# Reordered roundings, clips and turns in an expert stage, with its weights loaded in 2 MB DMAs

## The chip, the cores and the metric

The kernel runs on one core of a Trainium2 chip. The metric is the device time of the whole program in microseconds (us), the median of several runs.

## The reference, cut to what matters

One layer of a hybrid encoder on 512 tokens of width 1024, in float32. Three token mixers (differential attention, an mLSTM, a cross-attention into 256 memory tokens) are gated, projected and added; then comes a mixture of experts, the part that the change touches:

```python
h = h + mix @ w_out
xt = rms_norm(h)                                  # (512, 1024)
top_v, top_i = lax.top_k(xt @ router_w + router_b, 4)     # 4 of 32 experts for each token
top_w = softmax(top_v)
h1 = ragged_dot(xt[tok], w_gate_up) + b_gate_up   # each expert: 1024 x 2048
gate, up = minimum(h1[:, :1024], 7), clip(h1[:, 1024:], -7, 7)
a = (up + 1) * gate * sigmoid(1.702 * gate)
y = (ragged_dot(a, w_down) + b_down) * top_w      # each expert: 1024 x 1024
out = h + segment_sum(y, tok)
```

Each expert has 12 MB of weights, all 32 together 384 MB. Each must be read once from HBM.

## The kernel before, in words

The mixers and their projections fill the first half of the time (`stage_prep` to `stage_mix`) and are the same in both kernels but for the first expert loads. `stage_moe` (L2179) does the experts, one after the other.

**Order of the experts.** The router's counts sort the experts into seats: `KINDS_OF` (L61) says for each place in the sequence whether it is big (0, up to 128 tokens) or small (1, up to 64 tokens). Place 0 and place 31 are big; between them stand 15 pairs, a small one and then a big one (`pairs`, L2526). Expert numbers are read from `K.order` at run time.

**Units.** The weights of an expert are cut into 12 units of 1 MB, [128 x 2048] float32, at the positions `pos` 0 to 3 (up), 4 to 7 (down), 8 to 11 (gate). For each position there is one slot in SBUF, `moe_raw` (L2962), so 12 slots hold exactly one expert's amount. The slots 0 and 1, 2 and 3, and so on are neighbours in SBUF (`homes`, L2960).

**Small experts** use a slot as it is: `small_unit` (L2301) multiplies in full float32, two column halves of 64 tokens at a time, straight from `moe_raw`.

**Big experts** are split: ScalarE rounds a unit to float32r into `moe_hi` (`hi`, L2230, a ring of six), VectorE writes the remainder over the raw slot as `moe_lo` (`lo`, L2237), and TensorE does three products for each piece (`unit`, L2285): 12 matmuls of 512 columns a unit. So each unit of a big expert needs first ScalarE, then VectorE, then TensorE. The split units of a big expert are counted by `off` 0 to 11 in the order of use: up 0 to 3, gate 4 to 7, down 8 to 11 (`place`, L2252).

**Order on each engine**, written out by hand. TensorE, for an expert n (`small`, L2578, and `big`, L2595): the up units of n; behind the second of them the turn (transpose) of the activations `a` of expert n-1 (`turn_a`, L2383); the down units of n-1; the gate units of n; behind the second of them the turn of the gathered rows of n+1 (`turn_x`, L2330). ScalarE (L2670 to L2694): in `small` the Silu of expert n-1, rounding 8 of it, `keep_a_hi` (the rounded turned activations), roundings 9 to 11, the weighting of y, `keep_x_hi` of the next expert and its roundings 0 and 1; in `big` the Silu of the small expert before it, `keep_a_small` (L2458), roundings 2 to 5, the weighting, rounding 6, `keep_x_small` (L2412), rounding 7. VectorE (L2817 to L2840) follows with swiglu, remainders, and `clip` (L2428), which frees the banks of the up product.

**Loads.** SP (`refill`, L2537) goes through the positions in the order 0 to 11, which is the order in which TensorE uses them. For each it waits until the unit in the slot has been used (`s_use`, counted by TensorE once a unit), and loads the next 1 MB (`load`, L2225): rows of 8 KB, one for each of the 128 partitions. Positions 0 to 3 and 8 to 11 are loaded for expert n+1, positions 4 to 7 for expert n, whose down part comes one expert later. Each slot has a semaphore of its own. The first four units are loaded by `stage_mix` at L1727, the others of the first expert at L1734.

**Gather and scatter.** POOL gathers the rows of the next expert from HBM (`fetch`, L2489) and adds the weighted results into the output with an indirect DMA (`late`, L2507).

The first wait of `keep_a_small`, for TensorE's turn of `a`, and what stands behind it on ScalarE:

```python
def keep_a_small(act, n):
    act.wait_ge(s_aT, START + n * 2 + 2)
...
    silu(act, n - 1, 0, 2)
    keep_a_small(act, n - 1)
    for off in (2, 3, 4, 5):
        big_hi(act, n, off)
```

Of the kernel before, what the change touches and what calls it, by code (L numbers as in the profile page):

```python
# [33 lines left out]
ds = bass.ds  # L34

P = 128
# [1565 lines left out]
def stage_mix(K, ctx):  # L1602
# [92 lines left out]
    @block.sync  # L1695
    def _(sp):


        def pairs(q):
            for i in range(RING):  # L1700
                sp.wait_ge(s_y if i % 2 else s_g, q * 2 + (i // 2 - 1))
                refill(K, sp, q + Q0, i)
        with sp.Fori(1, CA0 // RING + 1) as q:
            pairs(q)

        sp.wait_ge(s_y, KT)
        sp.dma_start(h1, A["x"].rearrange("(t p) d -> p t d", p=P)).then_inc(s_x, 16)
        with sp.Fori(CA0 // RING + 1, ML0 // RING + 1) as q:
            pairs(q)
        sp.wait_ge(s_y, 2 * KT)  # L1710
        sp.dma_start(wx.rearrange("p (u n) -> p u n", u=4),
                     A["w_units"][4 * Q0 + OUT0 + 4:4 * Q0 + OUT0 + 8].rearrange("u p n -> p u n")).then_inc(s_wx, 16)
        with sp.Fori(0, 2) as it:
            for u in range(12):
                s = it * 4 + u // 3
                if u % 3 == 1:
                    sp.wait_ge(s_half, s + 1)
                else:
                    sp.wait_ge(s_y if u % 3 else s_g, s + (2 * KT + 1))
                refill(K, sp, *unit(it * 3 + (ML0 // RING + 1 + Q0), u))  # L1720
        for dst, name in ((braw[0:NE, :], "b_gu"), (braw[NE:2 * NE, :], "b_gu"), (gf[:], "g_ffn"), (rw[:], "rw"),
                          (rbias[:], "rb"), (eb[:], "eb"), (tri[:], "tri"), (iota[:], "iota"),
                          (tokf[:], "tokf"), (lim[:], "lim"), (bdn[0:NE, :], "b_dn"), (bdn[NE:2 * NE, :], "b_dn"),
                          (bdn[2 * NE:3 * NE, :], "b_dn"), (K.rec[:], "rec"),
                          (K.orec[:], "orec"), (K.moe_pick[:], "pick"), (sort[:], "sort")):
            sp.dma_start(dst, A[name]).then_inc(s_c, 16)
        for u in range(4):  # L1727
            sp.dma_start(K.moe_raw[u][:], A["w_moe"][u]).then_inc(K.s_moew[u], 16)
        sp.dma_start(K.lists.rearrange("(p r) f -> p (r f)", p=P), A["fill"]).then_inc(K.s_fill, 16)
        sp.dma_start(K.over, A["ove"]).then_inc(K.s_fill, 16)  # L1730
        for t in range(TT):
            sp.wait_ge(s_hn, t + 1)
            sp.dma_start(K.hn_d[t * P:(t + 1) * P, :], hn[:, t, :]).then_inc(s_hd, 16)
        for u in (8, 9, 10, 11, 4, 5, 6, 7):  # L1734
            sp.wait_ge(s_o, 2 * TT)
            sp.dma_start(K.moe_raw[u][:], A["w_moe"][u]).then_inc(K.s_moew[u], 16)

    @block.tensor
    def _(pe):
# [151 lines left out]
    def _(act):  # L1891
# [55 lines left out]
            op.then_inc(s_trk, 1)  # L1947

        def moe_hi(u):
            act.wait_ge(K.s_moew[u], 16)  # L1950
            act.wait_ge(s_o, TT)
            nc.scalar.activation(K.moe_hi[u][:], K.moe_raw[u][:], ACT.Copy).then_inc(s_mhi, 1)

# [225 lines left out]
def stage_moe(K, ctx):  # L2179
# [1 line left out]
    nc, A = K.nc, K.A  # L2181
    sb = lambda n, s, dt=F32: K.sb("moe_" + n, s, dt, ctx=ctx)
    HF, U = FF // 2, 4 * (FF // 2)
    RAW, LO, HI, s_w, s_LG, s_Xg = K.moe_raw, K.moe_lo, K.moe_hi, K.s_moew, K.s_LG, K.s_Xg
    b0, b1 = K.base[K.xcT.name] + 4 * 2 * U, K.base[K.yH.name] + 4 * KT * S
    a, y = K.place("moe_a", FF, b0), K.place("moe_y", D, b0 + 4 * FF)
    um, sg = K.place("moe_um", FF, b0 + 8 * FF), K.place("moe_sg", FF, b0 + 12 * FF)
# [36 lines left out]

    def load(sp, e, pos):  # L2225

        sp.dma_start(RAW[pos][:], A["w_moe"][ds(e * 12 + pos, 1)].rearrange("o p n -> (o p) n")
                     ).then_inc(s_w[pos], 16)

    def hi(act, ring, pos, arrived, free):  # L2230

        act.wait_ge(s_w[pos], arrived)
        if free is not None:
            act.wait_ge(s_use, free)  # L2234
        nc.scalar.activation(HI[ring][:], RAW[pos][:], ACT.Copy).then_inc(s_hi, 1)  # L2235
# [26 lines left out]
    def big_lo(dve, b, off):  # L2262

        lo(dve, nth(b, off), off % 6, place(off))
# [35 lines left out]

    def small_unit(pe, pos, arrived, bank, xs, k0, start, stop):  # L2301

        pe.wait_ge(s_w[pos], arrived)
        for kk in range(2):
            for j in range(2):
                mm = nc.tensor.matmul(half(bank, j), xs(k0 + kk), RAW[pos][:, cut(kk, j)], start=start and kk == 0,  # L2306
                                      stop=stop and kk == 1)
        mm.then_inc(s_use, 1)
# [225 lines left out]
    with nc.Block(no_gpsimd_drain=True) as block:  # L2534
        @block.sync
        def _(sp):
            def refill(n, first=False):  # L2537

                here, ahead = None if first else expert(sp, n), expert(sp, n + 1)
                for pos in range(12):  # L2540
                    if first and pos in DOWN:
                        continue
                    sp.wait_ge(s_use, count(n, pos))
                    load(sp, here if pos in DOWN else ahead, pos)
                    if first and pos == 3:
                        sp.wait_ge(s_h1, 2 * TT)
                        sp.dma_start(A["out"].rearrange("(t p) d -> p t d", p=P), h1).then_inc(K.s_acc, 16)

            refill(0, True)
            with sp.Fori(1, NE - 1) as n:  # L2550
                refill(n)
            here = expert(sp, NE - 1)
            for pos in DOWN:
                sp.wait_ge(s_use, count(NE - 1, pos))
                load(sp, here, pos)

            def item(i, n):
                e = sp.value_load(K.over_sb[0:1, ds(i * 2, 1)], min_val=0, max_val=NE - 1)
                sp.wait_ge(s_use, i * 12 + B)
                for pos in ORDER:  # L2560
                    load(sp, e, pos)
            overflow(sp, item, lambda: sp.wait_ge(K.s_ov, 20 * 16))
            sp.wait_ge(s_sc, 16 * NE)

        @block.tensor
        def _(pe):
# [11 lines left out]
            def small(n, it):  # L2578
                up_ready(pe, n)
                small_bias(1, UP[0], 0)  # L2580
                for p in small_part(n, 0, UP[0]):
                    if p == 1:
                        turn_a(pe, n - 1, 0)
                        turn_a(pe, n - 1, 1)
                for p in range(4):
                    if p % 2 == 0:
                        down_ready(pe, n - 1, p // 2)
                    unit(pe, nth(it, 8 + p), (8 + p) % 6, 4 + p, Yb, aTh, aTl, 2 * p, p == 0, p == 3)
                gate_ready(pe, n)
                small_bias(1, GATE[0], 2)  # L2590
                for p in small_part(n, 8, GATE[0]):
                    if p == 1:
                        turn_x(pe, n + 1)

            def big(n, b, last):  # L2595
                up_ready(pe, n)
                bias(0, UP, 0)
                for p in big_part(n, b, 0, UP, 0):
                    if p == 1:
                        turn_a(pe, n - 1, 0, 2)  # L2600
                down_ready(pe, n - 1, 1)
                for p in range(4):
# [66 lines left out]
        def _(act):  # L2669
            def small(n, it):  # L2670
# [6 lines left out]
                    big_hi(act, n - 1, off)  # L2677
                weigh(act, n - 1)
                keep_x_hi(act, n + 1, 0)
                for off in (0, 1):  # L2680
                    big_hi(act, n + 1, off)

            def big(n, b, last):
                silu(act, n - 1, 0, 2)
                keep_a_small(act, n - 1)
                for off in (2, 3, 4, 5):
                    big_hi(act, n, off)
                weigh_small(act, n - 1)
                big_hi(act, n, 6)
# [126 lines left out]
        def _(dve):  # L2816
            def small(n, it):  # L2817
# [6 lines left out]
                for off in (9, 10, 11):  # L2824
                    big_lo(dve, it, off)
                keep_x_lo(dve, it + 1, 0)
                for off in (0, 1):
                    big_lo(dve, it + 1, off)

            def big(n, b, last):  # L2830
                swiglu(dve, n - 1, 0, 2)
                for off in (2, 3, 4):
                    big_lo(dve, b, off)
                for h in range(2):
                    clip(dve, n, h)
                for off in (5, 6):
                    big_lo(dve, b, off)
                if last:
                    keep_x_lo(dve, b + 1, 1)
                big_lo(dve, b, 7)  # L2840
# [60 lines left out]
def program(nc, A):  # L2901
    with ExitStack() as ctx:
# [17 lines left out]
        with ExitStack() as c0:  # L2920
# [9 lines left out]
            with ExitStack() as c1:  # L2930
                K.memH, K.memL = (K.sb(n, [P, KT, M], R32, ctx=c1) for n in ("memH", "memL"))
                with ExitStack() as c2:
# [26 lines left out]
            U = 4 * (FF // 2)  # L2959
            homes = [K.base[K.xnH.name] + 4 * U * j for j in range(4)] + [K.base[K.mixH.name] + 4 * U * j for j in range(4)] + \  # L2960
                    [K.base[K.y_caT.name] + 4 * U * j for j in range(2)] + [K.base[K.yH.name] + 4 * U * j for j in range(2)]
            K.moe_raw = [K.place(f"moe_raw{j}", U, at) for j, at in enumerate(homes)]  # L2962
            K.moe_lo = [K.rounded(f"moe_lo{j}", K.moe_raw[j]) for j in range(12)]
            homes = [K.base[wraw.name] + 4 * U * j for j in range(4)] + [K.base[K.xcT.name] + 4 * U * j for j in range(2)]
            K.moe_hi = [K.place(f"moe_hi{j}", U, at, R32) for j, at in enumerate(homes)]
            K.moe_Xg = K.place("moe_Xg", D, K.base[K.sg[0].name])
            K.s_moew = [nc.alloc_semaphore(f"moe_unit{j}") for j in range(12)]
            K.s_acc, K.s_fill, K.s_ov, K.s_LG, K.s_Xg = (nc.alloc_semaphore(n) for n in (
                "moe_acc", "lists_empty", "over_listed", "moe_list", "moe_gathered"))
            stage_mix(K)  # L2970
# [5 lines left out]
def layouts(x, mem, attn_norm_g, w_in, b_gate, da_q_norm_g, da_k_norm_g, da_lambda_q1, da_lambda_k1,  # L2976
# [86 lines left out]
    moe = np.empty((NE, 3, 4, P, 2, FF), np.float32)  # L3063
    for i, w in enumerate((gu[..., 1, :], dn, gu[..., 0, :])):
        moe[:, i] = w.transpose(0, 1, 3, 2, 4)
    out["w_moe"] = moe.reshape(NE * 12, P, 4 * HF)
    out["b_gu"] = np.asarray(b_gate_up)[0].reshape(NE, 2, FF)[:, ::-1].reshape(NE, 2 * FF)
    out["b_dn"] = np.asarray(b_down)[0]
    pick = np.zeros((P, NE), np.float32)
# [20 lines left out]
```

## Time and profile before

| | us |
|---|---|
| median of 3 runs | 2281.13 |
| lowest, highest | 2278.28, 2285.19 |
| the profiled execution, its own time | 2283.67 |
| its span, first to last instruction | 2282.1 |
| mean granted TensorE clock in the span | 0.955 of full speed |

TensorE's clock has two levels, 1.2 and 2.4 GHz; a granted clock of 1.00 in a stretch is the upper one throughout, 0.50 the lower one. In the timelines PE is TensorE's matmuls, ACT is ScalarE, DVE is VectorE, SPq the sequencer of SyncE that issues the loads. The bracket at the end of a line is the idle time of the engine just before it and what ended it. Matmuls overlap in the pipeline, so the distance from one start to the next says more than the length of one. DMA share is the busy share of the core's 16 DMA engines; it can go slightly over 1 where packets of two queues overlap.

### The profile page before, as it was taken

How to read it: one execution, taken by the hardware profiler on the slowest of the kernel's cores; microseconds unless marked ns; L12 is line 12 of the kernel's file. 1: busy time of each engine (PE TensorE's matmuls, PEld its weight loads, DVE VectorE, ACT ScalarE, POOL GpSimd, SP SyncE). 2: the span in 40 equal slices, each digit the busy share in tenths (PEclk: the TensorE clock that was granted, in tenths of full speed). 3: DMA queues.
4: the chain of work that ended last, by engine and by line, in shares of the span. 5: the costliest groups of instructions: out<-in, count | busy, mean ns of one | idle time of the engine just before them, and what ended most of it. 6: DMA issues, size and time to landing. Idle time of an engine off the chain costs nothing.

```text
span 2282.1 us, 28033 instructions
## 1 busy us (share of the span) xinstructions
PE 2089.6 (92%) x9488; PEld 1487.5 (65%) x9488; DVE 1121.6 (49%) x1406; ACT 947.4 (42%) x1334; POOL 300.8 (13%) x398
## 2 busy tenths in 40 slices
PE   7999899999999999998988889888988889888986
PEld 6888677776667888887655555555555555555555
DVE  6777345654444344346543544444443544444454
ACT  5666443342224333234343443434443443434353
POOL 3334100202220000001101010111101010111100
PEclk9999999999999999997999999999999999999998
DMA  4110332311113424254999999899999898898962
GB/s 184 56 55 28 120 102 91 119 58 36 47 37 121 137 92 139 92 175 194 378 358 349 357 379 356 343 346 359 380 356 350 341 389 347 349 353 342 389 257 84
DMA packets 87093, 515.99 MB, mean 226 GB/s; under 512 B 13124, under 2 KB 14148, under 8 KB 36264
## 3 DMA queue, kind: packets, MB, share of 16 engines
q1 hardware_dynamic: 79448, 498.30, 57.4%
q0 software_dynamic: 7296, 16.79, 3.0%
q8 instruction: 37, 0.61, 0.1%
q14 instruction: 24, 0.20, 0.0%
q10 hardware_dynamic: 288, 0.09, 0.0%
HBM read 504.91 MB, written 19.40 MB: 230 GB/s over the span
## 4 chain that ended last, share of the span: by engine, by line
PE 32%; ACT 7%; DVE 7%; issue 6%; ACTq 0%; POOL 0%; POOLq 0%
PE bank L2306 9%; PE bank L2292 7%; DVE moe_lo L2240 7%; ACT moe_hi L2235 6%; PE bank L2294 6%; PE bank L2293 6%; PE bank L2327 1%; PE bank L2336 1%; PE bank L2389 0%; PE bank L2322 0%; ACT moe_XTh L2402 0%; ACT moe_XTs L2417 0%; ACTq L2234 0%; DVE moe_um L2433 0%; ACT moe_aTh L2450 0%
## 5 line engine op out<-in xcount | busy, mean ns | idle before, releaser
L2240 DVE TENSOR_TENSOR moe_lo<-moe_raw,moe_hi 128x2048 fp32r<-128x2048 f32 x202 | 455.5, 2290 | 278.4 <-ACT moe_hi L2235 221.6
L2235 ACT ACTIVATE moe_hi<-moe_raw 128x2048 fp32r<-128x2048 f32 x200 | 371.4, 1911 | 6.5 <-PEq L136 2.6
L2292 PE MATMUL bank<-moe_hi,moe_XTh 128*128 128x512 f32 x540 | 236.2, 437 | 128.1 <-DVE moe_lo L2240 128.1
L2294 PE MATMUL bank<-moe_hi,moe_XTl 128*128 128x512 f32 x540 | 228.1, 422 | 0.0
L2293 PE MATMUL bank<-moe_lo,moe_XTh 128*128 128x512 f32 x540 | 227.2, 421 | 0.0
L179 DVE TENSOR_TENSOR unit_lo<-unit_raw,unit_hi 128x1024 fp32r<-128x1024 f32 x116 | 145.2, 1257 | 164.2 <-ACT unit_hi L173 163.9
L173 ACT ACTIVATE unit_hi<-unit_raw 128x1024 fp32r<-128x1024 f32 x116 | 122.3, 1060 | 243.1 <-DMA unit_raw<-in_w_units 237.2
L2292 PEld LDWEIGHTS bank<-moe_hi,moe_XTh 128*128 128x128 f32 x540 | 111.5, 206 | 168.9 <-DVE moe_lo L2240 145.9
L2306 PE MATMUL bank<-moe_raw,moe_XTs 128*64 128x512 f32 x960 | 217.7, 595 | 0.0
L2514 POOL DMA_INDIRECT out<-moe_y,moe_LS x32 | 49.3, 1541 | 772.3 <-ACT moe_y L2475 389.2
L2306 PEld LDWEIGHTS bank<-moe_raw,moe_XTs 128*64 128x64 f32 x960 | 66.1, 137 | 126.4 <-issue 126.4
L2294 PEld LDWEIGHTS bank<-moe_hi,moe_XTl 128*128 128x128 f32 x540 | 111.1, 206 | 26.2
L2293 PEld LDWEIGHTS bank<-moe_lo,moe_XTh 128*128 128x128 f32 x540 | 112.6, 209 | 23.1
L2292 PE MATMUL bank<-moe_hi,moe_aTh 128*128 128x512 f32 x272 | 111.5, 410 | 10.0 <-DVE moe_lo L2240 6.0
L2293 PE MATMUL bank<-moe_lo,moe_aTh 128*128 128x512 f32 x272 | 107.8, 396 | 0.0
L2294 PE MATMUL bank<-moe_hi,moe_aTl 128*128 128x512 f32 x272 | 107.3, 394 | 0.0
L2306 PE MATMUL bank<-moe_raw,moe_aTs 128*64 128x512 f32 x480 | 106.3, 595 | 0.0
L2408 DVE TENSOR_TENSOR moe_XTl<-bank,moe_XTh 128x512 fp32r<-128x512 f32 x34 | 21.9, 687 | 165.9 <-ACT moe_XTh L2402 165.9
L1749 PE MATMUL bank<-yH,unit_hi 128*128 128x512 f32 x256 | 100.4, 392 | 2.3 <-DVE mix_da_lo L1640 2.3
L1751 PE MATMUL bank<-yH,unit_lo 128*128 128x512 f32 x256 | 100.5, 393 | 0.0
L393 PE MATMUL bank<-da_slab_hi,xnH 128*128 128x384 f32 x256 | 92.8, 362 | 4.6 <-DVE xnL L214 4.6
L2481 ACT ACTIVATE moe_y<-bank,moe_LS 64x512 f32<-64x512 f32 x30 | 20.6, 686 | 181.6 <-PE bank L2306 181.2
(399 smaller groups left out, 3866.5 us busy)
## 6 DMA issues: line engine op xcount, KB each, us to landing
moe_raw<-in_w_moe SPq DMA_DIRECT2D x384, 1024.0 KB, 7.8
unit_raw<-in_w_units SPq DMA_DIRECT2D x116, 512.0 KB, 3.6
da_slab<-in_w_qkv SPq DMA_DIRECT2D x8, 1536.0 KB, 6.8
y_caT<-in_x SPq DMA_DIRECT2D x4, 512.0 KB, 5.8
yda_d<-y_daT SPq DMA_DIRECT2D x1, 2048.0 KB, 6.3
y_daT<-in_blocks_qk SPq DMA_DIRECT2D x1, 2048.0 KB, 11.1
y_daT<-yda_d SPq DMA_DIRECT2D x1, 2048.0 KB, 8.2
y_daT<-in_x SPq DMA_DIRECT2D x1, 2048.0 KB, 8.6
```

Source lines behind the costliest of these rows:

```text
L173: K.nc.scalar.activation(K.whi[:, i, :], K.wraw[:, i, :], ACT.Copy).then_inc(K.s_whi, 1)
L179: K.nc.vector.tensor_tensor(K.wlo[:, i, :], K.wraw[:, i, :], K.whi[:, i, :].bitcast(F32), ALU.subtract).then_inc(K.s_wlo, 1)
L393: nc.tensor.matmul(bank, xh, wh, start=(k == 0), stop=False)
L1749: nc.tensor.matmul(bank[:], whi[:, i, w], hi[:, x], start=(k0 + k == 0), stop=False)
L1751: mm = nc.tensor.matmul(bank[:], wl, hi[:, x], start=False, stop=(k0 + k == depth - 1))
L2235: nc.scalar.activation(HI[ring][:], RAW[pos][:], ACT.Copy).then_inc(s_hi, 1)
L2240: nc.vector.tensor_tensor(LO[pos][:], RAW[pos][:], HI[ring][:].bitcast(F32), ALU.subtract).then_inc(s_lo, 1)
L2292: nc.tensor.matmul(banks[j][:], xh[:, x], HI[ring][:, w], start=start and kk == 0, stop=False)
L2293: nc.tensor.matmul(banks[j][:], xh[:, x], LO[pos][:, w], start=False, stop=False)
L2294: mm = nc.tensor.matmul(banks[j][:], xl[:, x], HI[ring][:, w], start=False, stop=stop and kk == 1)
L2306: mm = nc.tensor.matmul(half(bank, j), xs(k0 + kk), RAW[pos][:, cut(kk, j)], start=start and kk == 0, stop=stop and kk == 1)
L2514: nc.gpsimd.indirect_dma_start(A["out"], bass.IndirectOffsetOnAxis(ap=LS[0:rows, 0:1], axis=0), y[0:rows, :], None, bounds_check=S - 1, oo ...
```

## The change

Four things, all around the expert stage:

- Loads: the 12 slots are also seen as six double slots (`moe_two`) of neighbouring positions. The weights lie in HBM so that the two units of a double slot stand side by side in a row: 16 KB for each partition, 2 MB in one DMA. SP waits for the odd position of each double slot alone. There are six semaphores for twelve, so whoever needs one half waits for the whole.
- ScalarE: rounding 1 of a big expert moves from the end of `small` to behind the Silu in `big`; roundings 2 and 3 move ahead of `keep_a_small`.
- VectorE: remainder 1 moves behind the swiglu in `big`, and remainder 5 ahead of the two clips.
- TensorE: in `big` the turn of `a` comes behind the third up unit, not the second; in `small` the first of the two turns stays behind the second up unit, the other one comes behind the third.

```diff
@@ stage_mix, SP: the first loads @@
-        for u in range(4):
-            sp.dma_start(K.moe_raw[u][:], A["w_moe"][u]).then_inc(K.s_moew[u], 16)
+        for u in range(2):
+            sp.dma_start(K.moe_two[u][:], A["w_moe"][u]).then_inc(K.s_moew[u], 16)
...
-        for u in (8, 9, 10, 11, 4, 5, 6, 7):
+        for u in (4, 5, 2, 3):
             sp.wait_ge(s_o, 2 * TT)
-            sp.dma_start(K.moe_raw[u][:], A["w_moe"][u]).then_inc(K.s_moew[u], 16)
+            sp.dma_start(K.moe_two[u][:], A["w_moe"][u]).then_inc(K.s_moew[u], 16)
@@ stage_mix, moe_hi; the same index in hi and small_unit of stage_moe @@
-            act.wait_ge(K.s_moew[u], 16)
+            act.wait_ge(K.s_moew[u // 2], 16)
@@ stage_moe, load @@
-        sp.dma_start(RAW[pos][:], A["w_moe"][ds(e * 12 + pos, 1)].rearrange("o p n -> (o p) n")
-                     ).then_inc(s_w[pos], 16)
+        sp.dma_start(TWO[pos // 2][:], A["w_moe"][ds(e * 6 + pos // 2, 1)].rearrange("o p n -> (o p) n")
+                     ).then_inc(s_w[pos // 2], 16)
@@ stage_moe, SP @@
-                for pos in range(12):
+                for pos in range(1, 12, 2):
...
-            for pos in DOWN:
+            for pos in DOWN[1::2]:
...
-                for pos in ORDER:
+                for pos in ORDER[0::2]:
@@ stage_moe, PE, small @@
                 for p in small_part(n, 0, UP[0]):
-                    if p == 1:
-                        turn_a(pe, n - 1, 0)
-                        turn_a(pe, n - 1, 1)
+                    if p in (1, 2):
+                        turn_a(pe, n - 1, p - 1)
@@ stage_moe, PE, big @@
                 for p in big_part(n, b, 0, UP, 0):
-                    if p == 1:
+                    if p == 2:
                         turn_a(pe, n - 1, 0, 2)
@@ stage_moe, ACT, end of small and big @@
                 keep_x_hi(act, n + 1, 0)
-                for off in (0, 1):
-                    big_hi(act, n + 1, off)
+                big_hi(act, n + 1, 0)
 
             def big(n, b, last):
                 silu(act, n - 1, 0, 2)
+                for off in (1, 2, 3):
+                    big_hi(act, n, off)
                 keep_a_small(act, n - 1)
-                for off in (2, 3, 4, 5):
+                for off in (4, 5):
                     big_hi(act, n, off)
@@ stage_moe, DVE, end of small and big @@
                 keep_x_lo(dve, it + 1, 0)
-                for off in (0, 1):
-                    big_lo(dve, it + 1, off)
+                big_lo(dve, it + 1, 0)
 
             def big(n, b, last):
                 swiglu(dve, n - 1, 0, 2)
-                for off in (2, 3, 4):
+                for off in (1, 2, 3, 4, 5):
                     big_lo(dve, b, off)
                 for h in range(2):
                     clip(dve, n, h)
-                for off in (5, 6):
-                    big_lo(dve, b, off)
+                big_lo(dve, b, 6)
@@ program @@
-            K.moe_raw = [K.place(f"moe_raw{j}", U, at) for j, at in enumerate(homes)]
-            K.moe_lo = [K.rounded(f"moe_lo{j}", K.moe_raw[j]) for j in range(12)]
+            K.moe_two = [K.place(f"moe_two{j}", 2 * U, at) for j, at in enumerate(homes[0::2])]
+            K.moe_raw = [K.moe_two[j // 2][:, j % 2 * U:(j % 2 + 1) * U] for j in range(12)]
+            K.moe_lo = [K.rounded(f"moe_lo{j}", K.moe_two[j // 2], U, j % 2 * U) for j in range(12)]
...
-            K.s_moew = [nc.alloc_semaphore(f"moe_unit{j}") for j in range(12)]
+            K.s_moew = [nc.alloc_semaphore(f"moe_two{j}") for j in range(6)]
@@ layouts @@
-    out["w_moe"] = moe.reshape(NE * 12, P, 4 * HF)
+    out["w_moe"] = moe.reshape(NE * 6, 2, P, 4 * HF).transpose(0, 2, 1, 3).reshape(NE * 6, P, 8 * HF)
```

## Rows read from the trace of the kernel before

**Rows 1.** The page, part 1, busy time (share of the span) and count of instructions.
```profile
PE 2089.6 (92%) x9488; PEld 1487.5 (65%) x9488; DVE 1121.6 (49%) x1406; ACT 947.4 (42%) x1334; POOL 300.8 (13%) x398
```

**Rows 2.** Stretches: us, busy PE, PEld, DVE, ACT, POOL, then PEclk, DMA share, GB/s.
```profile
1139.20:2165.80 1026.60, 908.85 (x3921) 550.61 (x3921) 465.87 (x309) 427.86 (x377) 109.85 (x141) 0.94 0.93 358
1506.10:1579.00 72.90, 64.47 (x281) 39.14 (x281) 33.26 (x23) 30.65 (x27) 7.79 (x11) 0.95 0.93 359
1579.00:1652.80 73.80, 65.40 (x280) 39.52 (x280) 33.21 (x23) 30.65 (x27) 7.74 (x11) 0.93 0.92 352
```

**Rows 3.** The waits of PE from 1139.2 to 2165.8: total, times, longest.
```profile
PE bank L2292 <- DVE moe_lo L2240: 118.8, 56, 4.9
```

**Rows 4.** Timeline of PE, 1500 to 1560: start, us, what, [idle before].
```profile
1504.18 0.73 PE L2322 MATMUL bank<-moe_bias,moe_sel 128*128 128x512 f32 x2
1506.06 0.50 PE L2292 MATMUL bank<-moe_hi,moe_XTh 128*128 128x512 f32 x1 [1.15 <-DVE moe_lo L2240]
...
1511.64 0.60 PE L2389 MATMUL bank<-ident,moe_a 128*128 128x128 f32 x4
1517.10 0.79 PE L2292 MATMUL bank<-moe_hi,moe_XTh 128*128 128x512 f32 x1 [4.86 <-DVE moe_lo L2240]
...
1522.38 0.49 PE L2292 MATMUL bank<-moe_hi,moe_XTh 128*128 128x512 f32 x1
...
1544.38 0.50 PE L2292 MATMUL bank<-moe_hi,moe_XTh 128*128 128x512 f32 x1 [2.20 <-DVE moe_lo L2240]
...
1548.23 3.60 PE L2306 MATMUL bank<-moe_raw,moe_XTs 128*64 128x512 f32 x16
```

**Rows 5.** Timeline of PE, one pair later, 1590 to 1596.
```profile
1590.01 0.79 PE L2292 MATMUL bank<-moe_hi,moe_XTh 128*128 128x512 f32 x1 [4.86 <-DVE moe_lo L2240]
...
1594.02 0.52 PE L2292 MATMUL bank<-moe_hi,moe_XTh 128*128 128x512 f32 x1
```

**Rows 6.** Timeline of ACT, 1500 to 1525.
```profile
1500.80 1.09 ACT L2402 ACTIVATE moe_XTh<-bank 128x512 fp32r<-128x512 f32 x2 [4.29 <-PE bank L2336]
1501.77 3.71 ACT L2235 ACTIVATE moe_hi<-moe_raw 128x2048 fp32r<-128x2048 f32 x2
1505.37 0.59 ACT L2426 ACTIVATE moe_sg<-bank 128x512 f32<-128x512 f32 x1
1512.32 0.60 ACT L2462 ACTIVATE moe_aTs<-bank 128x512 f32<-128x512 f32 x1 [6.36 <-issue]
1512.82 7.31 ACT L2235 ACTIVATE moe_hi<-moe_raw 128x2048 fp32r<-128x2048 f32 x4
```

**Rows 7.** Timeline of DVE, 1500 to 1525.
```profile
1503.71 4.53 DVE L2240 TENSOR_TENSOR moe_lo<-moe_raw,moe_hi 128x2048 fp32r<-128x2048 f32 x2 [0.51 <-ACT moe_hi L2235]
1508.17 0.68 DVE L2443 SCALAR_TENSOR_TENSOR moe_a<-moe_sg,moe_um 128x512 f32<-128x512 f32 x1
1514.75 6.70 DVE L2240 TENSOR_TENSOR moe_lo<-moe_raw,moe_hi 128x2048 fp32r<-128x2048 f32 x3 [5.91 <-ACT moe_hi L2235]
```

**Rows 8.** Stretches again, for the last two columns, DMA share and GB/s.
```profile
1517.50:1525.00 7.50, 7.50 (x23) 5.88 (x23) 3.95 (x2) 2.62 (x2) 0.00 (x0) 0.66 0.28 92
1525.00:1575.00 50.00, 47.58 (x220) 27.22 (x220) 20.33 (x15) 18.98 (x20) 5.11 (x8) 1.00 1.00 398
1575.00:1583.00 8.00, 6.85 (x31) 4.06 (x27) 6.24 (x5) 3.87 (x3) 2.70 (x3) 1.00 1.01 323
395.00:400.00 5.00, 5.00 (x24) 4.14 (x23) 4.86 (x7) 2.28 (x4) 0.37 (x1) 1.00 0.98 326
400.00:405.00 5.00, 2.55 (x12) 1.82 (x12) 4.86 (x6) 0.63 (x1) 4.69 (x5) 1.00 1.00 415
```

**Rows 9.** SP's timeline, one load issued for the second slot of a pair.
```profile
1499.82 0.33 SPq L2227 DMA_DIRECT2D moe_raw<-in_w_moe  x1
```

**Rows 10.** The instructions and DMAs on moe_raw, the line on landings.
```profile
DMA to landing us min/median/max: 4.7/7.8/14.2
```

**Rows 11.** DMA issues: what, queue, count, median us from issue to landing.
```profile
moe_Xg<-hn_d,moe_LG POOLq DMA_INDIRECT x31, 9.0
```

More of the change, by code:

```diff
@@ L2183, in stage_moe @@
     HF, U = FF // 2, 4 * (FF // 2)
-    RAW, LO, HI, s_w, s_LG, s_Xg = K.moe_raw, K.moe_lo, K.moe_hi, K.s_moew, K.s_LG, K.s_Xg
+    RAW, TWO, LO, HI, s_w, s_LG, s_Xg = K.moe_raw, K.moe_two, K.moe_lo, K.moe_hi, K.s_moew, K.s_LG, K.s_Xg
     b0, b1 = K.base[K.xcT.name] + 4 * 2 * U, K.base[K.yH.name] + 4 * KT * S
@@ L2225, in load @@
     def load(sp, e, pos):
-        sp.dma_start(RAW[pos][:], A["w_moe"][ds(e * 12 + pos, 1)].rearrange("o p n -> (o p) n")
-                     ).then_inc(s_w[pos], 16)
+        sp.dma_start(TWO[pos // 2][:], A["w_moe"][ds(e * 6 + pos // 2, 1)].rearrange("o p n -> (o p) n")
+                     ).then_inc(s_w[pos // 2], 16)
     def hi(act, ring, pos, arrived, free):
-        act.wait_ge(s_w[pos], arrived)
+        act.wait_ge(s_w[pos // 2], arrived)
         if free is not None:
@@ L2301, in small_unit @@
     def small_unit(pe, pos, arrived, bank, xs, k0, start, stop):
-        pe.wait_ge(s_w[pos], arrived)
+        pe.wait_ge(s_w[pos // 2], arrived)
         for kk in range(2):
```

## The prediction, on record before the changed kernel ran

> **What bounds the kernel now.** I read the page first for the engines: TensorE is busy 2089.6 of 2282.1 us [rows 1]. Then the stretches: from the second expert on the expert stage is a rhythm of pairs, a small expert and a big one. The 14 whole pairs between 1139.2 and 2165.8 us take 1026.6 us, 73.33 us each, at a mean granted clock of 0.94, with the DMA engines 0.93 busy at 358 GB/s [rows 2]. Two resources are thus nearly full, and the question is which of them ends a pair.
>
> The list of waits says that TensorE loses 118.8 us of that stretch to one thing, the rounding remainder `moe_lo` [rows 3], which is 8.5 us a pair. No wait for a weight DMA stands there. The timeline of one pair shows where [rows 4]: 1.15 us before the first up unit of the big expert, 4.86 us before its third, 2.20 us before its last gate unit; the remaining 0.2 to 0.3 us are in the small expert. The 4.86 us wait has a tail: its matmuls run at half speed. Two units (24 matmuls) take 5.58 us from 1506.06 to 1511.64, so 12 take 2.79; the 12 behind the wait take 5.28 us (1517.10 to 1522.38), 2.49 us too much. In the pair behind, nine are slow and take 4.01 us instead of 2.09, 1.92 too much [rows 5]. I take 2.2 us a pair.
>
> Why 4.86? ScalarE's queue [rows 6]: after the Silu at 1505.37 it stands before `keep_a_small`, which needs TensorE's turn of `a`, put behind the second up unit. It starts at 1512.32, and only behind it come the roundings of the third unit (1512.82, 1.9 us), VectorE's remainder at 1514.75 (2.3 us, [rows 7]), and TensorE at 1517.10. A circle: TensorE turns, then waits for two roundings that nobody was kept from doing earlier but by the order of the queue.
>
> The DMA engines are no bound yet: while TensorE stands and runs slowly they run dry, share 0.28 from 1517.5 to 1525 (5.4 us idle), since all slots are full; after that they stay full, 398 GB/s over 50 us and 323 GB/s in the 8 us in which scatter and gather run beside them [rows 8].
>
> **The change, part by part.**
>
> *Order in the big expert.* In the times of the pair shown. Rounding 0 stays: ScalarE 1501.77 to 1503.7, VectorE 1503.71 to 1506.0, first up unit at 1506.06. Rounding 1 now comes behind the Silu, which needs the end of the small gate (about 1504.4: the next thing on TensorE, a bias product, begins at 1504.18, its predecessor's last matmul ends then). Silu 0.6 to 1505.05, rounding 1.9 to 6.95, remainder 2.3 to 9.3; VectorE's swiglu (0.68) fits in before it, at 1506.0. The first unit ends at 1508.85, so the second waits 0.45, call it 0.5: a new wait. Rounding 2 ends 1508.85 and its remainder 1511.6, while unit 1 runs to 1512.1; rounding 3 and its remainder end at 1513.9, before unit 2 ends at 1514.85. Then the turn (0.5), unit 3 to 1518.1, while `keep_a_small` (0.6) ends at 1516.0, ahead of the small down part. So the down part starts at 1518.1 instead of 1525.3. What is late next: roundings 4 and 5 come 16.0 to 19.8 on ScalarE, remainders to 22.5, then the clips, before TensorE needs unit 4 at 1525.9. The 2.20 us before the last unit stay: its rounding still stands behind `keep_x_small`.
>
> *Order in the small expert.* The second turn moves behind the third unit (1.8 us, two take 3.60 [rows 4]). ScalarE's `keep_a_hi` for it and rounding 9 come about 1.8 us later; remainder 9 waited for the clip, which waits for the whole up part, and still does. Cost 0; if that cover were gone, 1.8 us at most a pair.
>
> *Sum on TensorE's side.* A pair goes from 73.33 by -4.86 -2.2 +0.5 to 66.8 us, -6.56. The wait of 4.86 us stands in all 15 pairs: 98 us.
>
> *2 MB loads.* SP issues half as many DMAs (0.33 us each [rows 9], hidden). Each waits for the odd slot of its pair, one unit later for the even one (1.8 us small, 2.75 big), and nothing else is queued behind it that would be due earlier, since SP's order is the order of use. Both halves are there only when 2 MB are, one more 1 MB (2.6 us at 398 GB/s) for the even one. The tightest is the pair of the big expert's first gate units: its second slot is freed and loaded at 1499.82 [rows 9], landings take 7.8 us in the middle and 14.2 at most [rows 10], so 1507.6 to 1514.0, with the extra 1 MB up to 1516.6. ScalarE wants it at 1516.0, TensorE needs it by 1525.9 less 4.2 for the two roundings, 1521.7. So 5 to 14 us of lead. Others are landed 10 us and more ahead: the first pair is freed at 1512.1 and used half a period later. I price the coarser slots at nothing, covered by this lead.
>
> *Does DMA then set the pace?* A pair moves 358 x 73.33 = 26.25 MB. With the engines full the rate is (50 x 398 + 8 x 323) / 58 = 388 GB/s [rows 8], 67.7 us a pair, 0.9 more than TensorE's 66.8. Walking the new issue times (1504.4, 1512.1, 1518.1, 1521.7, 1525.3, 1531.5, 1540, then 1544.8, 1549, 1555, 1561, 1565.5) against 5.3 us for each 2 MB, the queue has 2 to 3 us of work left at every issue: it never runs dry, so DMA can really give its 67.7. Fifteen pairs fall 15 x 0.9 = 14 us behind; the lead takes up 5 to 14 of it, I take 9.5, so 4.5 us are lost: 94 us are left.
>
> *The rows of 16 KB.* Nothing in this stage has them; the nearest rows are the stretch in which a 2 MB tile with rows of 16 KB arrives: 415 GB/s at share 1.00 (400 to 405 us), and 326 at 0.98 just before it, where small rows arrive too [rows 8]. Against 398 for 8 KB rows that is no clear gain or loss; I take 0, as the cleaner stretch is above 398, and keep 326 for the slow side. As for the upper side, at 415 a pair of 67.7 us would be 65, and TensorE's 66.8 would hold throughout (98 us).
>
> *Elsewhere.* The first four units and the last eight before the stage come as two and four DMAs; TensorE waits there for the routing. At the end of the stage the last down units are loaded in pairs too; one more unit and 1 MB of delay there, 2.75 + 2.6, would cost 5 us once, and I take 0, since four gate units of 2.75 us lie between. The gather (9.0 us to landing [rows 11]) may take longer between 16 KB rows; it has 25 us until the turn of the next expert's rows. All else 0.
>
> **Against a page.** The trace shows 398 GB/s held for 50 us [rows 8]. The Trainium skill, page "DMA: Bandwidth & Descriptors", section "Where 436 GB/s comes from", says that for HBM to SBUF the HBM side binds at about 358 GB/s for a core. By that rule a pair could not go under 26.25 MB / 358 = 73.3 us and the change would bring nothing. That the stretch's mean is exactly 358 looks like agreement; the 50 us stretch speaks against it, and this program runs on one core.
>
> **The number.** The profiled execution took 2283.67 us, 1.6 more than its span and 2.5 above the median of 2281.13; less 94 it would be 2190, from the median 2187. I give 2187.
>
> **Rivals.**
> 1. *DMA never runs dry before, but does with 2 MB.* If my 2 to 3 us of queued work are not there, each pair lets the engines stand for one big unit, 2.75 us, on top of 67.7: 70.45, gain 2.9 x 15 = 43, 2238 us. For: the walk's margin is as small as that. Against: landings of 7.8 us mean nearly 3 MB queued. 0.13.
> 2. *A ceiling at today's mean rate of 358 GB/s*: each pair's freed time goes into waits for landings, 73.3 us stays: 2281 us, no change. Against: rows 8. 0.04.
> 3. *The stall moves, not goes*: another wait takes its place (rounding 1 behind the Silu, or 4 and 5 behind `keep_a_small`), or the order on a queue is not what I read. It would need 6.5 us instead of 0.5. 2281 us. 0.03.
> 4. *Slower: rows of 16 KB are slow.* If they run at 326 / 0.98 = 333 GB/s, as in the stretch at 395 us, a pair takes 26.25 / 333 = 78.8 us, +5.5 x 15 = 82: 2363 us. It decides from the point where the full rate falls under 26.25 / 73.33 = 358 GB/s. Against: 415 right behind it. 0.05.
>
> **Chances and range.** The forecast, 0.66: TensorE's or DMA's pace within 66.8 to 67.7. Its own range: 98 us and no slow matmuls behind the 2.20 us wait (the pairs of 72.90 and 73.80 us [rows 2] differ by that; 0.45 x 15 = 7) give 2176; DMA's pace with no lead is 15 x 5.6 = 84, and 7 more for a clock that falls each time, 2204. Another 0.09 lies just outside, on the fast side or between this and rival 1. Range to 2225 toward rival 1, 2172 below. About 0.3% (7 us) is what a measurement can tell. Faster: 0.66 + 0.09 + 0.13 + 0.02 of the cases at no change = 0.90; same 0.05; slower 0.05.
>
> **What would show it.** Right: no 4.86 us wait and no row of slow matmuls in the up part; a short wait of about 0.5 us before the second up unit; 2.20 still there; DMA share about 1.0 with no hole; pairs of 66.8, later ones a little longer with a wait for a landing before gate unit 4 of the big expert; `moe_raw` issued 192 times with 2048 KB. Wrong: pairs over 68 us, holes in the DMA share, waits for landings in the first pairs, or a full share at under 380 GB/s.

## The result, and the profile after

| | before | after |
|---|---|---|
| median of the runs, us | 2282.51 (4 runs, 2278.28 to 2285.19) | 2186.43 (4 runs, 2183.73 to 2186.74) |
| the profiled execution, us | 2283.67 | 2186.66 |
| its span, us | 2282.1 | 2185.1 |
| mean granted clock | 0.955 | 0.976 |

The ratio is 0.9578, 95% interval 0.9561 to 0.9596: 96 us less. The forecast was 2187. The number is right; some of its terms are not, and they happen to cancel nearly, as the experiments show.

The page of the changed kernel: engines, the slices of 55 us for the DMA engines, and the weight loads, now 192 of 2 MB.

```profile
PE 2062.0 (94%) x9488; PEld 1461.8 (67%) x9488; DVE 1124.0 (51%) x1406; ACT 949.9 (43%) x1334; POOL 308.0 (14%) x398
...
DMA  4110232320112343334599999999999999999972
GB/s 192 58 58 29 97 116 78 136 74 29 49 39 97 96 135 104 127 96 163 226 386 406 392 393 400 385 401 385 389 395 395 385 406 383 388 390 392 388 302 87
...
moe_two<-in_w_moe SPq DMA_DIRECT2D x192, 2048.0 KB, 10.9
```

The stretches that answer to [rows 2]: 14 whole pairs, then one pair with slow matmuls and one without. Columns are as there, the last three being PEclk, DMA share and GB/s.

```profile
1139.60:2075.70 936.10, 884.52 (x3920) 527.63 (x3920) 467.21 (x309) 430.79 (x378) 119.78 (x141) 0.99 0.99 392
1540.20:1607.70 67.50, 63.85 (x280) 38.03 (x280) 33.36 (x23) 30.85 (x28) 9.81 (x11) 0.97 0.98 389
1607.70:1673.70 66.00, 62.30 (x280) 37.10 (x280) 33.37 (x23) 30.86 (x28) 8.14 (x11) 1.00 1.00 395
```

A pair takes 936.1 / 14 = 66.87 us instead of 73.33. That is 6.46 less, times 15 pairs 96.9 us, if the last pair gains as the other 14 do: the whole difference of the spans (97.0). The DMA share went from 0.93 to 0.99, so of the hole of 5 us in each pair less than 1 us is left.

TensorE's waits in that stretch, which answer to [rows 3], and its timeline in one pair, to [rows 4]:

```profile
PE bank L2292 <- DVE moe_lo L2240: 49.9, 43, 2.2
```
```profile
1540.21 0.50 PE L2292 MATMUL bank<-moe_hi,moe_XTh 128*128 128x512 f32 x1 [1.15 <-DVE moe_lo L2240]
...
1542.84 0.39 PE L2294 MATMUL bank<-moe_hi,moe_XTl 128*128 128x512 f32 x1
1543.37 0.50 PE L2292 MATMUL bank<-moe_hi,moe_XTh 128*128 128x512 f32 x1
...
1548.99 0.60 PE L2389 MATMUL bank<-ident,moe_a 128*128 128x128 f32 x4
...
1552.29 6.23 PE L2306 MATMUL bank<-moe_two,moe_aTs 128*64 128x512 f32 x28
...
1571.34 0.50 PE L2292 MATMUL bank<-moe_hi,moe_XTh 128*128 128x512 f32 x1 [2.20 <-DVE moe_lo L2240]
...
1572.61 0.63 PE L2294 MATMUL bank<-moe_hi,moe_XTl 128*128 128x512 f32 x1
```

118.8 us of waiting have become 49.9, and the longest wait is 2.2 instead of 4.9. The 4.86 us wait before the third up unit is gone, and the down part starts 12.1 us behind the first up unit (1552.29); the prediction had worked out 12.0, and 19.2 before. Before the second unit (1543.37) a start is 0.53 us behind the last one instead of 0.23: the new wait, for rounding 1 behind the Silu, is 0.3 us. The wait of 2.20 is where it was, and behind it some matmuls of 0.63 us, at half speed, still appear.

ScalarE in the same pair, which answers to [rows 6]: roundings 1 to 3 in one piece behind the Silu, then `keep_a_small`, then 4 and 5.

```profile
1535.92 1.91 ACT L2235 ACTIVATE moe_hi<-moe_two 128x2048 fp32r<-128x2048 f32 x1
1538.59 0.60 ACT L2426 ACTIVATE moe_sg<-bank 128x512 f32<-128x512 f32 x1 [0.76 <-PE bank L2306]
1539.09 5.51 ACT L2235 ACTIVATE moe_hi<-moe_two 128x2048 fp32r<-128x2048 f32 x3
1549.67 0.60 ACT L2462 ACTIVATE moe_aTs<-bank 128x512 f32<-128x512 f32 x1 [5.08 <-issue]
1550.17 3.70 ACT L2235 ACTIVATE moe_hi<-moe_two 128x2048 fp32r<-128x2048 f32 x2
```

### The profile page after: what moved, and what is told of

Read it like the earlier page. It is cut to its first block and busy times, and to the rows that moved or that the text cites. A ratio compares the mean times of both kernels' runs of the same rounds, so it can differ in the third digit from the quotient of the medians.

```text
span 2185.1 us, 27289 instructions
## 1 busy us (share of the span) xinstructions
PE 2062.0 (94%) x9488; PEld 1461.8 (67%) x9488; DVE 1124.0 (51%) x1406; ACT 949.9 (43%) x1334; POOL 308.0 (14%) x398
## 5 line engine op out<-in xcount | busy, mean ns | idle before, releaser
L2240 DVE TENSOR_TENSOR moe_lo<-moe_two,moe_hi 128x2048 fp32r<-128x2048 f32 x202 | 455.0, 2288 | 231.4 <-ACT moe_hi L2235 229.7
L2235 ACT ACTIVATE moe_hi<-moe_two 128x2048 fp32r<-128x2048 f32 x200 | 372.8, 1908 | 6.5 <-PEq L136 2.6
L2292 PE MATMUL bank<-moe_hi,moe_XTh 128*128 128x512 f32 x540 | 224.6, 416 | 57.3 <-DVE moe_lo L2240 55.5
L2306 PE MATMUL bank<-moe_two,moe_XTs 128*64 128x512 f32 x960 | 221.0, 597 | 0.0
L2294 PE MATMUL bank<-moe_hi,moe_XTl 128*128 128x512 f32 x540 | 217.3, 402 | 0.0
L2293 PE MATMUL bank<-moe_lo,moe_XTh 128*128 128x512 f32 x540 | 216.7, 401 | 0.0
L2306 PEld LDWEIGHTS bank<-moe_two,moe_XTs 128*64 128x64 f32 x960 | 64.9, 137 | 119.0 <-issue 119.0
L2293 PEld LDWEIGHTS bank<-moe_lo,moe_XTh 128*128 128x128 f32 x540 | 104.7, 194 | 20.2
L2306 PE MATMUL bank<-moe_two,moe_aTs 128*64 128x512 f32 x480 | 106.3, 595 | 0.0
L1184 PE MATMUL bank<-xnH,unit_hi 128*128 128x512 f32 x232 | 94.6, 408 | 0.0
## 6 DMA issues: line engine op xcount, KB each, us to landing
moe_two<-in_w_moe SPq DMA_DIRECT2D x192, 2048.0 KB, 10.9
```

The source lines that it names most:

```text
L1184: nc.tensor.matmul(out, K.whi[:, i, w], K.xnH[:, k, :], start=(k == 0), stop=False)
L2240: nc.vector.tensor_tensor(LO[pos][:], RAW[pos][:], HI[ring][:].bitcast(F32), ALU.subtract).then_inc(s_lo, 1)
L2292: nc.tensor.matmul(banks[j][:], xh[:, x], HI[ring][:, w], start=start and kk == 0, stop=False)
L2293: nc.tensor.matmul(banks[j][:], xh[:, x], LO[pos][:, w], start=False, stop=False)
L2294: mm = nc.tensor.matmul(banks[j][:], xl[:, x], HI[ring][:, w], start=False, stop=stop and kk == 1)
```

## The experiments

The change has three parts: the order of the roundings, the places of the turns, and the loads. The questions were which of them bring the 96 us, and whether the DMA engines set the pace now. All times are medians of five runs (eleven for the second), each ratio against the kernel before on the same chip.

**1. The new order, with loads of 1 MB.** The order of the changed kernel on all engines; `load`, the semaphores and the layout as before. Against the changed kernel:

```diff
-        sp.dma_start(TWO[pos // 2][:], A["w_moe"][ds(e * 6 + pos // 2, 1)].rearrange("o p n -> (o p) n")
-                     ).then_inc(s_w[pos // 2], 16)
+        sp.dma_start(RAW[pos][:], A["w_moe"][ds(e * 12 + pos, 1)].rearrange("o p n -> (o p) n")
+                     ).then_inc(s_w[pos], 16)
...
-                for pos in range(1, 12, 2):
+                for pos in range(12):
```

> The new order with the 12 loads of 1 MB of the kernel before. Theory A (the whole gain is the order; the DMA engines with rows of 8 KB could give 388 GB/s, 67.7 us a pair, against TensorE's 66.87): between 2186 and 2198 us, the DMA share at 1.0, and in the later pairs waits for landings or a shrinking lead of the gate load over its rounding. Rival B (the shape of the loads plays no part at this pace): 2186 within 3 us, no wait for a landing anywhere. Rival C (the coarse loads carry a part of the gain): over 2205 us.

Measured: 2185.90 us, ratio 0.9580 (0.9567 to 0.9593). TensorE's waits, 1139.2 to 2070 us:

```profile
PE bank L2292 <- DVE moe_lo L2240: 48.5, 40, 2.2
```

That is the changed kernel's time and its list. No wait for a landing appears. The middle time from issue to landing of a 1 MB load is 8.6 us (7.8 before). Rival B is right: the shape of the loads plays no part at this pace. Theory A's waits for landings, and with them the step of the forecast that had the DMA engines fall behind, do not appear.

**2. The 2 MB loads alone**, with the order of before.

```diff
-                if p in (1, 2):
-                        turn_a(pe, n - 1, p - 1)
+                if p == 1:
+                        turn_a(pe, n - 1, 0)
+                        turn_a(pe, n - 1, 1)
...
-                for off in (1, 2, 3):
-                    big_hi(act, n, off)
                 keep_a_small(act, n - 1)
-                for off in (4, 5):
+                for off in (2, 3, 4, 5):
```

> The loads of 2 MB in rows of 16 KB with the order of before. Theory A: no change from the kernel before, 2282 within 5 us, the 4.86 us wait in all 15 pairs, the hole in the DMA share wider by what is faster. Rival C (coarse loads help by themselves): under 2270 us. Rival D (they come late where the lead is 1 to 3 us): over 2290 us.

Measured: 2283.54 us, ratio 1.0008 (0.9999 to 1.0017). No change, as theory A said. The stretch that answers to the first of [rows 2], and the wait:

```profile
1139.20:2165.80 1026.60, 909.16 (x3920) 550.81 (x3918) 465.07 (x308) 427.48 (x377) 108.44 (x140) 0.94 0.92 357
```
```profile
PE bank L2292 <- DVE moe_lo L2240: 117.7, 55, 4.9
```

**3. The changed kernel with rows of 8 KB** in the same 2 MB DMAs.

```diff
-        sp.dma_start(TWO[pos // 2][:], A["w_moe"][ds(e * 6 + pos // 2, 1)].rearrange("o p n -> (o p) n")
+        sp.dma_start(TWO[pos // 2][:].rearrange("p (u n) -> p u n", u=2),
+                     A["w_moe"][ds(e * 12 + pos // 2 * 2, 2)].rearrange("u p n -> p u n")
```

> The changed kernel with the weights laid out as before, so that the same 2 MB DMA consists of two rows of 8 KB for each partition. Theory A (rows of 8 KB cap at 388 GB/s): 2186 to 2198 us, later landings than in the changed kernel, the lead over the rounding of gate unit 4 shrinks from 1 to 3 us to nothing. Rival B (rows play no part): 2186 within 3 us, same leads.

Measured: 2188.61 us, ratio 0.9587 (0.9574 to 0.9600), middle landing 11.1 us against 10.9. The profiled execution of it has a span of 2183.6 us. Its interval overlaps the changed kernel's; a difference is not shown at this pace. Experiment 8 has one.

**4. The roundings and remainders alone**: the new order on ScalarE and VectorE, loads of 1 MB, turns where they were. Against experiment 1, on TensorE alone:

```diff
-                    if p in (1, 2):
-                        turn_a(pe, n - 1, p - 1)
+                    if p == 1:
+                        turn_a(pe, n - 1, 0)
+                        turn_a(pe, n - 1, 1)
...
-                    if p == 2:
+                    if p == 1:
                         turn_a(pe, n - 1, 0, 2)
```

> The kernel before with the order of ScalarE and VectorE alone changed (roundings 1 to 3, remainder 5); the turns stay behind the second up unit, the loads stay 1 MB. Theory A (the circle is broken by the roundings, the place of the turn is of no weight): within 3 us of the run with the full order and 1 MB loads. Rival E (the turn's place carries a part: the second up unit ends before a is there, or the turn delays keep_a_small's successors): over 5 us slower than that run.

Measured: 2180.01 us, ratio 0.9551 (0.9538 to 0.9564). Theory A had expected the time of experiment 1 within 3 us, rival E over 5 us more. It is 5.9 us *less*: breaking the circle takes the new order of roundings and remainders and nothing else, and the new places of the turns cost something. (Which of the roundings and remainders had to move was not tried one by one.) Where the turns cost, two timelines show. The changed kernel, small expert, from the second up unit on:

```profile
1512.72 0.66 PE L2389 MATMUL bank<-ident,moe_a 128*128 128x128 f32 x4
1513.31 1.94 PE L2306 MATMUL bank<-moe_two,moe_XTs 128*64 128x512 f32 x8
1515.17 0.66 PE L2389 MATMUL bank<-ident,moe_a 128*128 128x128 f32 x4
1515.76 1.94 PE L2306 MATMUL bank<-moe_two,moe_XTs 128*64 128x512 f32 x8
1517.63 0.50 PE L2292 MATMUL bank<-moe_hi,moe_aTh 128*128 128x512 f32 x1
```

and the same work in this experiment:

```profile
1508.62 1.09 PE L2389 MATMUL bank<-ident,moe_a 128*128 128x128 f32 x8
1509.65 3.65 PE L2306 MATMUL bank<-moe_raw,moe_XTs 128*64 128x512 f32 x16
1513.23 0.50 PE L2292 MATMUL bank<-moe_hi,moe_aTh 128*128 128x512 f32 x1
```

From the first turn to the first down matmul it takes 1517.63 - 1512.72 = 4.91 us against 1513.23 - 1508.62 = 4.61. The same instructions, cut once more, cost 0.30 us a pair, 4.5 us in 15. The rest of the 5.9 us may be slow matmuls: 9 of the first 14 pairs have them behind the 2.20 us wait in the profile of experiment 1, 7 in this one.

**5. The changed kernel with the small expert's turns together again.**

```diff
-                    if p in (1, 2):
-                        turn_a(pe, n - 1, p - 1)
+                    if p == 1:
+                        turn_a(pe, n - 1, 0)
+                        turn_a(pe, n - 1, 1)
```

> The changed kernel with the two turns of the small expert put together again behind its second up unit; the big expert's turn stays behind its third. Theory H (the split costs: TensorE switches to turns and back once more, 4.91 us instead of 4.61 in the two traces for the same work): 4 to 6 us less than the changed kernel, about 2181 us. Rival E (the later turn in the big expert is what costs): no change from the changed kernel.

Measured: 2178.11 us, ratio 0.9553 (0.9537 to 0.9569). The changed kernel itself, beside it on the same chip:

> The changed kernel itself once more, so that the runs beside it are compared on one chip: 2186 us within 3.

2186.01 us, 0.9577 (0.9564 to 0.9590). So 7.9 us less, and theory H's direction holds; the amount is more than its 4 to 6. The rest is the clock. Two neighbouring pairs of this run, and its 14 whole pairs:

```profile
1467.70:1533.40 65.70, 61.98 (x280) 37.19 (x280) 33.29 (x23) 30.78 (x28) 7.86 (x11) 1.00 1.00 400
1533.40:1600.70 67.30, 63.58 (x281) 38.15 (x281) 33.34 (x23) 30.83 (x28) 7.88 (x11) 0.97 0.99 389
...
1131.00:2059.50 928.50, 876.74 (x3922) 526.55 (x3918) 465.89 (x308) 429.38 (x377) 117.40 (x140) 0.99 1.00 395
```

Pairs with no slow matmuls behind the 2.20 us wait take 65.7 here against 66.0, the 0.3 of the cut. Pairs with them take 1.5 to 1.6 us more. In the changed kernel's profile 8 of the first 14 pairs are such, in this one 6. By that the 14 pairs should take 14 x 0.3 + 2 x 1.55 = 7.3 us less; they take 936.1 - 928.5 = 7.6 less. (The two spans, 2185.1 and 2174.6, differ by 10.5; 3 us of that lie ahead of the first pair, where the kernels are the same.) The 2.20 us wait is the same in every pair; what decides whether slow matmuls follow it is not shown.

The turn of the big expert stands behind the third up unit here and behind the second in experiment 4. The ratios are 0.9553 and 0.9551: its place costs nothing that can be seen, and rival E falls. (The loads differ as well, which experiments 1 and 2 found to make no difference at this pace.)

**6. Rounding 7 ahead of `keep_x`**, which takes away the cause of the 2.20 us wait, to see whether the DMA engines follow.

```diff
                 big_hi(act, n, 6)
+                big_hi(act, n, 7)
                 if last:
                     keep_x_hi(act, n + 1, 1)
                 else:
                     keep_x_small(act, n + 1)
-                big_hi(act, n, 7)
...
+                big_lo(dve, b, 7)
                 if last:
                     keep_x_lo(dve, b + 1, 1)
-                big_lo(dve, b, 7)
```

> The changed kernel, rounding and remainder 7 moved ahead of keep_x on ScalarE and VectorE, so that the 2.20 us wait before the last gate unit goes. TensorE's side: 2.20 less, and 1.0 us for the slow matmuls behind it, 63.7 us a pair. Theory A (DMA engines full: 392 GB/s is what rows of 16 KB give): the pair stays at 66.3 to 66.9 us, 2178 to 2187 us, and waits for landings appear in TensorE's or ScalarE's list. Rival F (the engines still have room, up to the 415 GB/s of a clean stretch): 64 us a pair, 2140 to 2150 us, no such waits.

Measured: 2159.69 us, ratio 0.9456 (0.9442 to 0.9470). Between the two: the engines had some room, but not all that was asked for. Waits of ScalarE for landings now appear; from 1459 to 1853 us, about six later pairs, they are:

```profile
ACT moe_hi L2235 <- DMA moe_two<-in_w_moe: 58.1, 18, 6.7
```

DMA is the bound there; experiment 7 shows how it becomes so.

**7. The same with loads of 1 MB** in rows of 8 KB: the diff of experiment 6 on the kernel of experiment 1.

> The same with loads of 1 MB. DMA is the bound here by theory A, and this is the price of the load's shape: if 1 MB loads in rows of 8 KB give 388 GB/s at most, a pair takes 67.7 us, 10 to 20 us more than the run with 2 MB. Rival B (shape plays no part): within 3 us of it.

Measured: 2157.78 us, ratio 0.9445 (0.9432 to 0.9458), the same as experiment 6. This profile shows the passage from one bound to the other best. Two of its early pairs and one later, then the four early pairs together and a stretch of about six later ones:

```profile
1202.00:1265.60 63.60, 62.07 (x281) 37.16 (x280) 33.38 (x23) 30.97 (x28) 9.29 (x11) 1.00 1.02 405
1329.10:1392.60 63.50, 61.97 (x281) 37.16 (x280) 33.37 (x23) 31.09 (x28) 9.31 (x11) 1.00 1.02 405
1523.20:1589.30 66.10, 62.30 (x280) 37.08 (x280) 33.11 (x23) 31.28 (x29) 9.63 (x11) 1.00 1.01 396
...
1134.60:1388.60 254.00, 247.92 (x1122) 148.63 (x1120) 133.27 (x88) 123.86 (x109) 37.02 (x40) 1.00 1.02 405
1459.00:1853.00 394.00, 373.32 (x1679) 221.98 (x1677) 197.31 (x132) 186.28 (x163) 57.21 (x60) 1.00 1.01 398
```

For four pairs TensorE runs at its own pace, 63.5 us. The slots filled ahead are used up meanwhile: 405 GB/s over 254 us is 102.9 MB, 2.1 less than four pairs of 26.25 MB. Then landings set the pace, 65.8 us. ScalarE's waits from 1459 to 1853 us name it, and the middle time from issue to landing is now 22.9 us instead of 8.6:

```profile
ACT moe_hi L2235 <- DMA moe_raw<-in_w_moe: 65.2, 33, 6.2
```

No such line exists in the changed kernel. The rate falls from 405 to 398 GB/s in the passage, in experiment 6 from 407 to 399. Had 405 lasted, a pair would take 26.25 / 405 = 64.8 us. Why it does not is not shown, so 398 is the rate found where landings are waited for, and not the most that the engines can move.

**8. The same with 2 MB in rows of 8 KB**: the diffs of experiments 3 and 6 together.

> The same with loads of 2 MB in rows of 8 KB. If the length of the rows is what counts, the time is that of the 1 MB run; if the number of DMAs is, it is that of the run with rows of 16 KB. Theory A: the rows, so as the 1 MB run within 3 us. Rival G: the DMAs, so as the 16 KB run within 3 us.

Measured: 2167.21 us, ratio 0.9502 (0.9489 to 0.9515), 7.5 us over experiment 6 and 9.4 over experiment 7, clear of both intervals. Both expectations are wrong: neither the length of the rows nor the number of DMAs counts alone. 1 MB in rows of 8 KB and 2 MB in rows of 16 KB are equal, 2 MB made of two rows 1 MB apart in HBM for each partition is slower. The same stretch of later pairs, first experiment 6, then this one:

```profile
1459.00:1853.00 394.00, 373.82 (x1682) 222.49 (x1680) 197.78 (x133) 185.57 (x162) 56.86 (x60) 1.00 1.00 399
```
```profile
1459.00:1853.00 394.00, 370.10 (x1662) 220.86 (x1660) 197.19 (x131) 183.36 (x160) 53.98 (x59) 1.00 1.00 395
```

The DMA share is 1.00 in both, and the rates are 395 against 399 GB/s. Why is not settled here. That each load reads from one contiguous piece in both equal cases, and from two in this one, is a difference, but no run tests it by itself.

**9. Rounding 0 ahead of `keep_x_hi` as well**, against the 1.15 us wait; on top of experiment 6, and the same on VectorE.

```diff
                 weigh(act, n - 1)
+                big_hi(act, n + 1, 0)
                 keep_x_hi(act, n + 1, 0)
-                big_hi(act, n + 1, 0)
```

> In addition rounding and remainder 0 ahead of keep_x in the small expert, so that the 1.15 us wait goes too. Theory A (DMA bound): the same time as with rounding 7 alone, within 4 us; the freed time turns into waits for landings. Rival F: 1.1 us less for each of 15 pairs, 17 us.

Measured: 2160.13 us, ratio 0.9464 (0.9450 to 0.9478), the same as experiment 6. That looks like theory A: ScalarE's waits for landings from 1459 to 1853 us are 70.8 us, against 58.1 in experiment 6. But TensorE had gained nothing that DMA could have taken away. The first three pairs, in which it still goes at its own pace, take 63.5 us each in both. Its timeline in one of them, from the bias products to the second up unit, first experiment 6, then this one:

```profile
1202.84 0.73 PE L2322 MATMUL bank<-moe_bias,moe_sel 128*128 128x512 f32 x2
1204.72 0.50 PE L2292 MATMUL bank<-moe_hi,moe_XTh 128*128 128x512 f32 x1 [1.15 <-DVE moe_lo L2240]
...
1207.87 0.50 PE L2292 MATMUL bank<-moe_hi,moe_XTh 128*128 128x512 f32 x1
```
```profile
1201.50 0.73 PE L2322 MATMUL bank<-moe_bias,moe_sel 128*128 128x512 f32 x2
1202.07 0.39 PE L2292 MATMUL bank<-moe_hi,moe_XTh 128*128 128x512 f32 x1
...
1206.54 0.51 PE L2292 MATMUL bank<-moe_hi,moe_XTh 128*128 128x512 f32 x1 [1.56 <-DVE moe_lo L2240]
```

The 1.15 us wait is gone, and a wait of 1.56 us stands one unit later, for the remainder of rounding 1, which comes behind the Silu. To the second unit it is 5.04 us against 5.03. So neither theory is tested by this run: rounding 1, which the change moved, holds the second unit where it was. Whether it could stay ahead of the Silu was not tried.

**10. The best of both**: loads of 1 MB, turns as before, roundings 1 to 3 early, rounding 7 ahead: the diff of experiment 6 on the kernel of experiment 4.

> Candidate for the best: 1 MB loads, turns as before, roundings 1 to 3 early, rounding 7 ahead of keep_x. TensorE has 0.3 us a pair less to do than in the run with 1 MB loads, split turns and rounding 7 first (2157.8 us). Theory A (DMA engines full, 401 GB/s): no gain from it, within 3 us. Rival (TensorE still sets the pace there): 4 to 5 us less, 2153 us.

Measured: 2157.26 us, ratio 0.9454 (0.9441 to 0.9466), with more waits for landings in the later pairs than in experiment 7:

```profile
ACT moe_hi L2235 <- DMA moe_raw<-in_w_moe: 84.0, 35, 8.9
```

It is 29 us under the changed kernel and no better than experiment 7: 0.3 us less work for TensorE shows in the early pairs (63.2 against 63.5 us) and is worth nothing where landings set the pace.

## Why the prediction was right, and where not

- **The circle: right.** 4.86 us gone in 15 of 15 pairs, ScalarE's order as worked out, the down part 12.1 us behind the first up unit against 12.0 forecast. Experiment 4 has it alone, without new turns or loads, and brings all of the gain and more.
- **The slow matmuls behind it: right**, gone (2.2 us a pair).
- **The new wait before the second up unit: mis-sized**, 0.3 us, not 0.5, which is 3.0 us too much in 15 pairs.
- **"Order in the small expert. ... Cost 0": wrong.** I looked at ScalarE and VectorE, where it does cost nothing, and did not price the cut on TensorE itself: 0.30 us a pair, 4.5 us (experiments 4 and 5).
- **The slow matmuls behind the 2.20 us wait** I left as they were, and nearly so they stayed: 7 of 14 pairs, every second one, have them before, 8 of 14 after. A pair with them takes 1.5 to 1.6 us more, so one more of them is 0.1 us a pair; the range had room for it.
- **"Does DMA then set the pace?": wrong.** I took 388 GB/s from 58 us of one pair as the ceiling, hence 67.7 us a pair and 4.5 us lost. Experiment 1 shows the old loads keeping up at 66.9, without the waits for landings that I expected in the later pairs. Experiments 6 and 7 show the engines at 405 to 407 GB/s over four pairs, and at 398 to 399 GB/s over 394 us, 65.7 to 65.8 us a pair, where landings are waited for. A share of 1.0 over less than one pair was not enough to read a ceiling from; why the rate was lower there is not shown. That leads get used up over some pairs before DMA decides was the right mechanism, one step too early: experiment 7 shows it.
- **The errors cancel**: 4.5 us too much for DMA and 3.0 too much for the new wait, against 4.5 too little for the cut turns. From the 94 of the forecast that leads to 94 + 4.5 + 3.0 - 4.5 = 97.0, and 96.9 were measured. The hit on 2187 is partly luck. With the measured terms a pair gains 4.86 + 2.2 - 0.3 (new wait) - 0.3 (cut) = 6.46 and loses 0.1 to the one slow pair more; that gives 6.35 of the 6.46 measured.
- **2 MB loads and 16 KB rows "at nothing": right**, shown by experiments 1, 2 and the pair 6 and 7. Rival 4 (slow rows of 16 KB) and rival 1 (DMA running dry) fall: 399 GB/s in experiment 6, and a share of 0.99 in the changed kernel. Rival 3 (the stall moves) falls with 66.87 us a pair.
- **The ceiling at 358 GB/s (rival 2) falls**: 392 GB/s over 936 us, 399 over 394 us in experiment 6. The Trainium skill, page "DMA: Bandwidth & Descriptors", section "Where 436 GB/s comes from", puts the limit at about 358 for HBM to SBUF; the measurement decides. This program has one core busy, and the same page's section "Measured" says that its higher figures hold for a core that streams alone.

## What to carry to other kernels

Where an in-order queue has a wait in front of work that is ready, look whether that wait ends a circle through another engine; moving two ready roundings (2 and 3) ahead of it, with the order of the remainders to match, was worth 4% here. A part of the change, the new places of the turns, was needless, and the one in the small expert cost 0.3 us each time. After a wait is removed, look one unit further on TensorE before the missing gain is put down to another resource: in experiment 9 the wait had only moved. Before loads are made larger, see whether anybody waits for a landing: with none in the list of waits, their shape was worth nothing, and when DMA did become the bound, 1 MB and 2 MB loads were equal as well, as long as each was one piece in HBM. A ceiling of a resource is best read from a kernel in which it is the bound, over several periods, not from one short stretch in a kernel where it is not.

## What the runs showed that was not expected

- A cut of eight turns into two times four, with a unit of matmuls between, costs 0.30 us of TensorE (4.91 against 4.61 us).
- One and the same wait of 2.20 us was followed by slow matmuls in some pairs and not in others (7 of 14 pairs before, 8 in the changed kernel, 6 in experiment 5). They do not fall by chance: two profiled executions of the changed kernel have them in the same pairs, the 2nd, 4th, 6th, 7th, 9th, 11th, 12th and 14th. With the wait gone (experiment 6) the clock is 1.00 throughout the pairs.
- A full DMA share went with different rates: 405 to 407 GB/s over the first four pairs, in which TensorE kept its own pace, 398 to 399 in the later ones, in one and the same execution (experiments 6 and 7).
- 2 MB loads made of two rows of 8 KB for each partition, 1 MB apart, run at 395 GB/s, 1% under the 399 of rows of 16 KB, and cost 7.5 us where DMA is the bound; 1 MB loads in rows of 8 KB do not (398).
